# Splitting the fifth expert's weight loads into a quarter, a quarter and a half of the first expert's up projection

## The chip, the cores and the metric

The kernel runs on one core of a Trainium2 chip. The metric is the device time of one execution in microseconds (us); lower is better. Each time is that of the whole program.

## The reference, cut to what matters

A decoder trunk of two layers over 256 tokens of width 1024, all in float32. Each layer is a mixer (gated linear recurrences, retention, a recurrent block) and a mixture of 32 experts; a final norm ends it. The part around the change is the mixture:

```python
def hier_moe(h, w_group, b_group, w_expert, b_expert, w1, w3, w2):
    ...
    top_v, top_i = lax.top_k(e_sel, MOE_TOPK)
    ...
    def expert_step(acc, p):
        w1e, w3e, w2e, ge = p
        hid = jax.nn.silu(xt @ w1e) * (xt @ w3e)
        return acc + ge[:, None].astype(xt.dtype) * (hid @ w2e), None
```

`w1` and `w3` are 1024 x 512 for each expert and `w2` is 512 x 1024, so an expert has 6.29 MB of weights and a layer's 32 experts have 201 MB.

## The kernel before

The two layers run one after the other. In each, the mixer's projections come first, then the final steps of its output projection, the routing (`route`), and then all 32 experts in order (`experts`). Every expert's weights are read from HBM, whatever the number of its tokens. An expert handles its tokens in passes of 32. One pass on TensorE is: gather the tokens (L1235), transpose (L1240, L1244), the up projection with `w1` and `w3` (L1259), the down projection with `w2` (L1275), and the scatter into the sums (L1286 or L1289). ACT and DVE work between these steps.

The up projection of a pass is a loop over eight chunks k of the width, with four calls in each, and each call shows in the trace as two matmul records: 64 records in a pass, 8 for each k. Chunk k reads column block k of `w1` and of `w3`; a whole `w1` is 16 KB in each of 128 partitions, so a half is 8 KB a partition and a quarter is 4 KB.

Weights lie in three slots of SBUF, used in turn. Expert 3 (`FOURTH`, counting from zero) has a place of its own, the memory of `x` and of lent constants, so the slot of expert 0 is next used by expert 4, the fifth (`FOURTH + 1`). All weight loads are issued by one queue, SP's, in an order written by hand: `first_experts` for those that go out during the mixer and the routing, then `load_experts`. There SP waits for a semaphore that tells that the slot was read, and then issues the loads into it. In `load_experts`, SP waits for the routing (`routed`), reads the first expert's token count and works out with `up_to(0)` how many passes there will have been (`done`). Then it waits until the first half of the up projection of that pass is done (`up_half_done`, given at k = 3) and issues the first halves of the fifth's `w1` and `w3`; waits for `up_done` and issues the second halves; waits for `down_done` and issues the fourth expert's `w2`. The next loads are those of expert 5 (L557), after the up projection of expert 1. Of the loop after that, SP's waits are L659 and L662.

Each load adds 16 to a semaphore when it has landed. The up projection waits for the count that `up_count(l, e)` works out; it knows how many loads an expert's weights came in (64 is four loads, 96 is six).

TensorE is kept active ahead of the last expert's up projection by some matmuls on zeros (`keep_warm`, L963), and the last expert's weights come in halves (`last_expert`). The next layer's mixer weights follow behind the last expert in the same queue.

Of the kernel before, what the change touches and what calls it, by code (L numbers as in the profile page):

```python
# [37 lines left out]
KC = D // P  # L38
# [12 lines left out]
PIECE = KC * 512  # L51
# [4 lines left out]
FOURTH = 3  # L56
# [85 lines left out]
def trunk(nc, x_in, even_w_in, even_w_out, odd_w_in, odd_w_out, gla_w_up, rglru_w_r, rglru_w_i,  # L142
# [7 lines left out]
    with ExitStack() as ctx:  # L150
# [3 lines left out]
        def sem(name):  # L154
            return ctx.enter_context(nc.semaphore(name))
# [54 lines left out]
        def up_slot(e):  # L210

            return ORDER[(e - (e > FOURTH)) % 3]

        def w1_place(e):

            return x_place if e == FOURTH else up_slot(e) * SLOT

        def w3_place(e):

            return lent_place if e == FOURTH else up_slot(e) * SLOT + PIECE  # L220
# [222 lines left out]
        got_scaled = sem("got_scaled")  # L443
        spread_turned = sem("spread_turned")
        spread_kept = sem("spread_kept")
        up_done, up_half_done = sem("up_done"), sem("up_half_done")
        fourth_up = Staged(sem("fourth_up"), 48)
        sums_begun = sem("sums_begun")
        silu_done = sem("silu_done")
# [10 lines left out]
        def up_count(l, e):  # L460

            def of(e):
                return 96 if e == 1 else 64 if e == FOURTH + 1 else 32

            same = [j for j in range(NE) if j != FOURTH and up_slot(j) == up_slot(e)]
            return l * sum(map(of, same)) + sum(of(j) for j in same if j <= e)
# [46 lines left out]
        def _(sp_q):  # L513
# [35 lines left out]
            def up_to(e):  # L549

                tokens = sp_q.value_load(counts[0:1, bass.ds(e, 1)], min_val=0, max_val=T)
                with sp_q.Fori(0, tokens, PASS):
                    sp_q.reg_add(passes, passes, 1)
                return sp_q.snap(passes, min_val=1, max_val=2 * NE * T // PASS)
# [9 lines left out]
            def load_half(l, e, src, place, half, loaded):  # L564

                part = slice(half * HALF, (half + 1) * HALF)
                sp_q.dma_start(at_place(place)[:, part], src[l, e].rearrange("(p k) f -> p (k f)", k=KC)[:, part]).then_inc(loaded, 16)
# [56 lines left out]
                sp_q.wait_ge(*((sums_begun, 1) if l == 0 else x_turned.at(1, 4)))  # L624
                load_half(l, FOURTH, moe_w1, x_place, 1, fourth_up.sem)

            def fifth_up(l, half):

                load_half(l, FOURTH + 1, moe_w1, w1_place(FOURTH + 1), half, up_loaded[up_slot(FOURTH + 1)])
                load_half(l, FOURTH + 1, moe_w3, w3_place(FOURTH + 1), half, up_loaded[up_slot(FOURTH + 1)])  # L630

            def load_experts(l):

                sp_q.wait_ge(*routed.at(l, 2))
                done = up_to(0)
                sp_q.wait_ge(up_half_done, done)
                fifth_up(l, 0)
                sp_q.wait_ge(up_done, done)
                fifth_up(l, 1)
                sp_q.wait_ge(down_done, done)  # L640
                load_down(l, FOURTH, ORDER[0])
                for e in (1, 2):
                    done = up_to(e)
                    sp_q.wait_ge(up_loaded[up_slot(e)], up_count(l, e))
                    sp_q.wait_ge(up_done, done)
                    load_up(l, e + 4, e + 4)
                    sp_q.wait_ge(down_loaded[ORDER[e]], down_count(l, e))
                    sp_q.wait_ge(down_done, done)
                    load_down(l, e + 3, ORDER[e])
                done = up_to(FOURTH)  # L650
                sp_q.wait_ge(down_loaded[ORDER[0]], down_count(l, FOURTH))
                sp_q.wait_ge(down_done, done)
                load_down(l, 2 * FOURTH, ORDER[0])
                with sp_q.Fori(0, (NE - 2 - 2 * FOURTH) // 3) as i:
                    for j in range(3):
                        e, like = 3 * i + (2 * FOURTH + 1 + j), 2 * FOURTH + 1 + j
                        done = up_to(3 * i + (FOURTH + 1 + j))
                        sp_q.wait_ge(up_loaded[up_slot(like)], up_count(l, like - 3) + 32 * i)
                        sp_q.wait_ge(up_done, done)  # L659
                        load_up(l, e, like)  # L660
                        sp_q.wait_ge(down_loaded[ORDER[like % 3]], down_count(l, like - 3) + 16 * i)
                        sp_q.wait_ge(down_done, done)  # L662
                        load_down(l, e, ORDER[like % 3])
                last_expert(l, NE - 1, up_to(NE - 4))
# [125 lines left out]
        def _(pe):  # L790
# [425 lines left out]
            def experts(l):  # L1216
# [7 lines left out]
                def expert(e, like, turn, passes):  # L1224
# [5 lines left out]
                    def body(base, n):  # L1230
# [24 lines left out]
                        for k in range(KC):  # L1255
                            if last and k == KC // 2:
                                pe.wait_ge(up_loaded[up_slot(like)], all_up)
                            for j in range(Q):
                                ins = pe.matmul(bank[2][PASS * j:PASS * (j + 1), 0:T], got_T[:, k % 2, k // 2, :],  # L1259
                                                up[:, k, :, j * P:(j + 1) * P], start=(k == 0), stop=(k == KC - 1),  # L1260
                                                tile_position=(0, PASS * j), skip_group_check=True)
                            if k == KC // 2 - 1:
                                ins.then_inc(up_half_done, 1)
                        ins.then_inc(up_done, 1)
# [976 lines left out]
```

## Time and the profile before

| what | value |
|---|---|
| time, median of 3 runs | 1135.0 us (1133.93 to 1135.4) |
| the profiled execution's own time | 1134.56 us |
| its span, first to last instruction | 1132.7 us |
| PE busy | 858.7 us, 76% |
| DVE busy | 354.8 us, 31% |
| ACT busy | 262.2 us, 23% |
| bytes read from HBM | 441.25 MB |
| mean rate over the span | 390 GB/s |
| mean granted clock of TensorE | 0.952 |

How to read it: busy shares are means over stages with different limits. The profiled execution's time is 1.9 us more than its span; that part lies outside the first and last instruction. The 16 DMA engines that move the weights are the resource with the highest share in the slices of the experts' stages.

### The profile page before, as it was taken

The page shows a single profiled execution, that of the slowest core. Times are in us where ns is not written, and L with a number is a line of the kernel's source. Part 1 is how long each engine was busy: PE and PEld are TensorE (multiplying, and loading weights), DVE is VectorE, ACT ScalarE, POOL GpSimd, SP SyncE. Part 2 cuts the span into 40 slices and gives each one's busy share as a digit, 9 for nine tenths or more (in the row PEclk, how much of TensorE's full clock was granted, in tenths as well). Part 3 has the DMA queues.
Part 4 walks back from the last instruction along what each step waited for, and adds up shares of the span by engine and source line. Part 5 has one row for each costly group of instructions (what it writes and reads, how often), then busy time and mean ns, then how long its engine had stood idle before and what let it go on. Part 6 is the DMA issues. An engine that isn't in the chain of part 4 may idle for free.

```text
span 1132.7 us, 25610 instructions
## 1 busy us (share of the span) xinstructions
PE 858.7 (76%) x10392; PEld 543.1 (48%) x10393; DVE 354.8 (31%) x841; ACT 262.2 (23%) x502; POOL 7.4 (1%) x16
## 2 busy tenths in 40 slices
PE   9999997777666666666779998777766666666665
PEld 8988964444333333333349896434433333333333
DVE  6898751212111111111128964121111111111112
ACT  7646541111100000000027744111100000100002
POOL 1000000000000000000001000000000000000000
PEclk9999999999998889999899999999999988988988
DMA  9744899999999999999999599999999999999996
GB/s 345 269 161 179 325 345 426 428 428 428 428 428 430 429 426 430 427 429 428 430 406 368 202 426 378 432 424 428 428 429 429 427 429 429 428 429 428 430 425 250
DMA packets 49901, 442.95 MB, mean 391 GB/s; under 512 B 4288, under 2 KB 5760, under 8 KB 23616
## 3 DMA queue, kind: packets, MB, share of 16 engines
q1 hardware_dynamic: 49584, 441.53, 94.0%
q8 instruction: 32, 0.52, 0.2%
q10 hardware_dynamic: 144, 0.52, 0.1%
q0 software_dynamic: 128, 0.26, 0.1%
q14 instruction: 13, 0.11, 0.0%
HBM read 441.25 MB, written 1.05 MB: 390 GB/s over the span
## 4 chain that ended last, share of the span: by engine, by line
DMA 47%; PE 38%; DVE 7%; ACT 4%; issue 3%; SPq 1%; DVEq 0%; ACTq 0%
DMA up_pairs<-in_moe_w_dram 43%; PE low_banks L1259 13%; PE low_banks L1275 4%; DMA weights<-in_moe_w_dram 4%; PE sums_of_x L812 3%; PE sums_of_x L814 3%; PE sums_of_x L813 3%; PE low_banks L1235 2%; DVE w_lo L1732 1%; PE low_banks L812 1%; PE sums_of_x L1286 1%; PE low_banks L813 1%; PE low_banks L814 1%; PE sums_of_x L1289 1%; PE low_banks L1027 1%
## 5 line engine op out<-in xcount | busy, mean ns | idle before, releaser
L1259 PE MATMUL low_banks<-up_pairs,gates 128*32 128x256 f32 x4096 | 277.4, 431 | 119.7 <-DMA up_pairs<-in_moe_w_dram 106.6
L1259 PEld LDWEIGHTS low_banks<-up_pairs,gates 128*32 128x32 f32 x4096 | 142.4, 123 | 239.1 <-DMA up_pairs<-in_moe_w_dram 116.9
L1275 PE MATMUL low_banks<-weights,gates 128*32 128x256 f32 x2048 | 124.0, 382 | 85.5 <-DVE gates L2153 53.8
L2151 DVE TENSOR_TENSOR gates<-gates,low_banks 128x128 f32<-128x128 f32 x64 | 18.4, 288 | 396.5 <-ACT gates L1321 396.5
L1275 PEld LDWEIGHTS low_banks<-weights,gates 128*32 128x32 f32 x2048 | 63.5, 109 | 145.9 <-issue 85.9
L1321 ACT ACTIVATE gates<-low_banks 128x128 f32<-128x128 f32 x64 | 17.8, 278 | 413.1 <-PE low_banks L1259 413.1
L2147 DVE TENSOR_TENSOR gates<-low_banks,vecs 128x256 f32<-128x256 f32 x64 | 27.2, 425 | 259.5 <-PE low_banks L1244 259.5
L1235 PE MATMUL low_banks<-tok,gates 128*32 128x256 f32 x1024 | 68.5, 385 | 15.0 <-issue 9.5
L1732 DVE TENSOR_TENSOR w_lo<-weights,w_hi 128x2048 fp32r<-128x2048 f32 x28 | 64.0, 2287 | 16.1 <-ACT w_hi L1392 15.9
L1563 ACT COPY gates<-low_banks 128x256 f32<-128x256 f32 x64 | 23.8, 372 | 191.3 <-PE low_banks L1275 191.3
L1557 ACT COPY gates<-low_banks 128x256 f32<-128x256 f32 x64 | 23.8, 372 | 159.2 <-PE low_banks L1235 159.2
L1392 ACT CAST w_hi<-weights 128x2048 fp32r<-128x2048 f32 x28 | 53.4, 1908 | 17.3 <-PE sums_of_x L814 12.2
L1235 PEld LDWEIGHTS low_banks<-tok,gates 128*32 128x32 f32 x1024 | 27.6, 109 | 50.6 <-issue 38.0
L2141 DVE TENSOR_SCALAR gates<-consts,y_T,scale 128x32 f32 x128 | 32.5, 299 | 57.3 <-issue 56.4
L1286 PE MATMUL sums_of_x<-gates 32*128 32x256 f32 x512 | 36.7, 400 | 15.6 <-ACT gates L1563 15.6
L1289 PE MATMUL sums_of_x<-gates 32*128 32x256 f32 x512 | 36.7, 400 | 15.6 <-ACT gates L1563 15.6
L2144 DVE TENSOR_SCALAR gates<-consts,y_T 128x128 f32 x128 | 38.4, 342 | 0.0
L1286 PEld LDWEIGHTS sums_of_x<-gates 32*128 32x128 f32 x512 | 23.1, 184 | 31.7 <-ACT gates L1563 31.0
L1289 PEld LDWEIGHTS sums_of_x<-gates 32*128 32x128 f32 x512 | 23.1, 184 | 31.7 <-ACT gates L1563 31.0
L1244 PE MATMUL low_banks<-consts,gates 128*128 128x128 f32 x128 | 28.0, 300 | 7.6
L812 PE MATMUL sums_of_x<-act_hi,w_hi 128*128 128x256 f32 x112 | 32.3, 288 | 1.0 <-DVE w_lo L1732 1.0
L812 PE MATMUL sums_of_x<-w_hi,act_hi 128*128 128x512 f32 x80 | 32.4, 404 | 0.0
(296 smaller groups left out, 1124.0 us busy)
## 6 DMA issues: line engine op xcount, KB each, us to landing
up_pairs<-in_moe_w_dram SPq DMA_DIRECT2D x114, 2048.0 KB, 33.6
weights<-in_moe_w_dram SPq DMA_DIRECT2D x60, 2048.0 KB, 39.6
up_pairs<-in_moe_w_dram SPq DMA_DIRECT2D x24, 1024.0 KB, 10.0
weights<-in_even_w_in_dram SPq DMA_DIRECT2D x5, 2048.0 KB, 11.2
weights<-in_odd_w_in_dram SPq DMA_DIRECT2D x4, 2048.0 KB, 21.6
weights<-in_moe_w_dram SPq DMA_DIRECT2D x6, 1024.0 KB, 38.0
up_pairs<-in_moe_w_dram SPq DMA_DIRECT2D x8, 512.0 KB, 9.0
weights<-in_even_w_in_dram SPq DMA_DIRECT2D x3, 1024.0 KB, 10.1
```

What stands on the lines that cost most here:

```text
L812: pe.matmul(dst, a_hi, b_hi, start=start, stop=False, skip_group_check=shared)
L813: pe.matmul(dst, a_hi, b_lo, start=False, stop=False, skip_group_check=shared)
L814: return pe.matmul(dst, a_lo, b_hi, start=False, stop=stop, skip_group_check=shared)
L1235: ins = pe.matmul(bank[0][PASS * q:PASS * (q + 1), 0:T], pick[:, a, :], tok[:, a, q * T:(q + 1) * T], start=(a == 0), stop=(a == TT - 1), ...
L1259: ins = pe.matmul(bank[2][PASS * j:PASS * (j + 1), 0:T], got_T[:, k % 2, k // 2, :], up[:, k, :, j * P:(j + 1) * P], start=(k == 0), stop= ...
L1275: ins = pe.matmul(bank[3][PASS * q:PASS * (q + 1), T:2 * T], hid_T[:, c, :], down[:, c, q * T:(q + 1) * T], start=(c == 0), stop=(c == Q - 1),
L1286: ins = pe.matmul(dst, y_tok[rows, part], spread_T[rows, :], start=False, stop=True, tile_position=(PASS * q, 0), skip_group_check=True)
L1289: ins = pe.matmul(dst, spread_T[rows, part], y_tok[rows, :], start=False, stop=True, tile_position=(PASS * q, 0), skip_group_check=True)
L1392: act.copy(hi, raw_w).then_inc(hi_set.sem, splits_of(l, i))
L1732: tt(lo, raw_w, hi.bitcast(F32), ALU.subtract).then_inc(lo_set.sem, splits_of(l, i))
L2141: ts(pick[:, a, :], numbers, place[:, a, bass.ds(e, 1)], scale[:, a:a + 1], ALU.is_equal, ALU.mult).then_inc(picked, 1)
L2144: ts(spread[:, a, :].rearrange("p (q s) -> p q s", q=Q), numbers.unsqueeze(1).to_broadcast([P, Q, PASS]), place[:, a, bass.ds(e, 1)], gate ...
```

## The change

The first expert's slot is given back in three parts and not in two. TensorE signals a new semaphore, `up_quarter_done`, at the end of chunk k = 1 of every pass, on a matmul that is there already. SP waits for it and issues the first quarter of the fifth expert's `w1` and `w3`, then waits for `up_half_done` and issues the second quarter of both, then for `up_done` and issues the second half of both. The bytes are the same: six loads (four of 512 KB, two of 1024 KB) instead of four of 1024 KB. `up_count` counts 96 for the fifth expert. This holds for both layers.

```diff
-        up_done, up_half_done = sem("up_done"), sem("up_half_done")
+        up_done, up_half_done, up_quarter_done = sem("up_done"), sem("up_half_done"), sem("up_quarter_done")
...
-                return 96 if e == 1 else 64 if e == FOURTH + 1 else 32
+                return 96 if e == 1 else 96 if e == FOURTH + 1 else 32
...
-            def fifth_up(l, half):
-
-                load_half(l, FOURTH + 1, moe_w1, w1_place(FOURTH + 1), half, up_loaded[up_slot(FOURTH + 1)])
-                load_half(l, FOURTH + 1, moe_w3, w3_place(FOURTH + 1), half, up_loaded[up_slot(FOURTH + 1)])
+            def fifth_up(l, first, last):
+
+                e = FOURTH + 1
+                part = slice(first * PIECE // KC, last * PIECE // KC)
+                for src, place in ((moe_w1, w1_place(e)), (moe_w3, w3_place(e))):
+                    sp_q.dma_start(at_place(place)[:, part], src[l, e].rearrange("(p k) f -> p (k f)", k=KC)[:, part]
+                                   ).then_inc(up_loaded[up_slot(e)], 16)
...
                 done = up_to(0)
+                sp_q.wait_ge(up_quarter_done, done)
+                fifth_up(l, 0, KC // 4)
                 sp_q.wait_ge(up_half_done, done)
-                fifth_up(l, 0)
+                fifth_up(l, KC // 4, KC // 2)
                 sp_q.wait_ge(up_done, done)
-                fifth_up(l, 1)
+                fifth_up(l, KC // 2, KC)
                 sp_q.wait_ge(down_done, done)
...
+                            if k == KC // 4 - 1:
+                                ins.then_inc(up_quarter_done, 1)
                             if k == KC // 2 - 1:
                                 ins.then_inc(up_half_done, 1)
```

## Rows read from the trace of the kernel before

**Rows 1.** The page: bytes moved in 40 equal slices of 28.3 us.
```profile
GB/s 345 269 161 179 325 345 426 428 428 428 428 428 430 429 426 430 427 429 428 430 406 368 202 426 378 432 424 428 428 429 429 427 429 429 428 429 428 430 425 250
```

**Rows 2.** The page: the chain that ended last, by engine.
```profile
DMA 47%; PE 38%; DVE 7%; ACT 4%; issue 3%; SPq 1%; DVEq 0%; ACTq 0%
```

**Rows 3.** The chain in order of time: start us, us, what.
```profile
163.92 3.66 PE low_banks L1259 x64
...
276.58 3.70 PE low_banks L1259 x64
280.93 36.00 DMA up_pairs<-in_moe_w_dram
...
697.81 3.66 PE low_banks L1259 x64
...
803.07 33.17 DMA up_pairs<-in_moe_w_dram
...
1060.86 39.65 DMA up_pairs<-in_moe_w_dram
1100.55 5.97 PE low_banks L1259 x64
```

**Rows 4.** Timeline of SP's queue, load issues: start us, us, line, count.
```profile
147.00 0.89 SPq L597 DMA_DIRECT2D up_pairs<-in_moe_w_dram  x2
...
165.91 2.71 SPq L567 DMA_DIRECT2D up_pairs<-in_moe_w_dram  x4
...
167.64 0.98 SPq L567 DMA_DIRECT2D up_pairs<-in_moe_w_dram  x2
...
170.76 0.33 SPq L574 DMA_DIRECT2D weights<-in_moe_w_dram  x1
178.71 1.48 SPq L557 DMA_DIRECT2D up_pairs<-in_moe_w_dram  x2
...
699.80 2.74 SPq L567 DMA_DIRECT2D up_pairs<-in_moe_w_dram  x4
...
712.51 0.80 SPq L557 DMA_DIRECT2D up_pairs<-in_moe_w_dram  x2
```

**Rows 5.** Windows, layer 0: length, engines' busy us, clock, DMA share, GB/s.
```profile
165.00:165.50 0.50, 0.50 (x16) 0.31 (x12) 0.00 (x0) 0.00 (x0) 0.00 (x0) 1.00 0.64 246
165.50:166.00 0.50, 0.50 (x16) 0.33 (x12) 0.00 (x0) 0.00 (x0) 0.00 (x0) 1.00 0.00 0
166.00:166.50 0.50, 0.50 (x16) 0.28 (x11) 0.00 (x0) 0.00 (x0) 0.00 (x0) 1.00 0.00 0
...
166.50:169.00 2.50, 1.30 (x25) 0.58 (x21) 0.69 (x2) 0.28 (x1) 0.00 (x0) 1.00 0.80 226
```

**Rows 6.** Windows, layer 1, the same columns.
```profile
699.00:699.50 0.50, 0.50 (x16) 0.30 (x12) 0.00 (x0) 0.00 (x0) 0.00 (x0) 1.00 0.55 229
699.50:700.00 0.50, 0.50 (x18) 0.27 (x10) 0.00 (x0) 0.00 (x0) 0.00 (x0) 1.00 0.24 98
700.00:700.50 0.50, 0.50 (x16) 0.33 (x12) 0.00 (x0) 0.00 (x0) 0.00 (x0) 1.00 0.23 98
...
700.50:703.00 2.50, 1.30 (x28) 0.61 (x24) 0.69 (x2) 0.28 (x1) 0.00 (x0) 1.00 0.85 239
```

**Rows 7.** Windows of longer stretches, the same columns.
```profile
154.00:157.00 3.00, 3.00 (x25) 2.90 (x25) 2.17 (x17) 2.87 (x5) 0.00 (x0) 1.00 1.05 405
147.00:150.00 3.00, 3.00 (x25) 2.34 (x25) 2.08 (x4) 1.26 (x2) 0.00 (x0) 1.00 1.03 434
165.50:178.70 13.20, 10.70 (x172) 5.65 (x164) 2.13 (x7) 1.41 (x5) 0.00 (x0) 1.00 0.89 357
699.50:712.50 13.00, 10.57 (x172) 5.57 (x160) 2.13 (x7) 1.41 (x5) 0.00 (x0) 1.00 0.94 371
189.60:277.00 87.40, 65.67 (x1000) 35.12 (x1004) 17.05 (x56) 10.91 (x32) 0.00 (x0) 1.00 1.01 427
...
178.70:181.70 3.00, 1.91 (x32) 1.13 (x32) 1.71 (x6) 0.23 (x1) 0.00 (x0) 1.00 1.02 431
```

**Rows 8.** Windows of the next-to-last expert's up projection in layer 1.
```profile
1100.50:1106.50 6.00, 5.91 (x64) 2.62 (x64) 0.00 (x0) 0.00 (x0) 0.00 (x0) 0.61 0.98 412
...
1115.90:1119.70 3.80, 3.72 (x66) 1.98 (x64) 0.00 (x0) 0.01 (x1) 0.00 (x0) 1.00 0.77 319
```

## The prediction

> **What bounds the kernel now.** I read the slices of the page first: from slice 7 on the core takes in 424 to 432 GB/s, nearly without a break, until layer 0's experts end, and again in layer 1 [rows 1]. That is the level of the DMA engines when they are full: 427 GB/s at a share of 1.01 over 87 us [rows 7]. The chain's summary says the same, 47% of the span for DMA against 38% for PE [rows 2]. The chain in order of time shows where which of the two holds: in layer 0 it runs on PE from the first expert until 280 us and then from one landing of weights to the next, and so in layer 1 from 803 us [rows 3]. The PE part of that chain is not a limit of its own. The stream of weights is full through it, and what the last landings wait for is the number of bytes ahead of them. So any time in which the DMA engines stand still after the stream has begun is paid again at each layer's end, and only such time can be won. There is one such hole in each layer, just where the change is made: in layer 0 the rate falls to 246 and then to 0 GB/s for a full microsecond [rows 5]; in layer 1 to 98 GB/s at a share of 0.24 for a microsecond, some engines still having work [rows 6]. Both end some 0.9 us after SP's four issues begin, at 165.91 and 699.80 us [rows 4].
>
> **The change part by part.**
>
> The moved issue. The four issues start when half of the first expert's up projection is done; the next two, which wait for its end, start 167.64 − 165.91 = 1.73 us later [rows 4]. Those 1.73 us are four chunks of k, so two chunks are 0.87 us, and the first quarter goes out at about 165.04 and 698.93 us. The up projection itself takes 3.66 us in both layers, one pass [rows 3], a quarter of which is 0.92 us; I take 0.87. SP is free by then: it has only been waiting. It issues two loads in 0.89 us [rows 4] (the pair at 147.00), so it is done at about 165.93 and comes some 0.02 us late to the half, nothing that counts, because 1.05 MB (2.5 us of transfer) is then ahead; the second half's issue stays at 167.64. Layer 0's hole, where all engines are idle, shortens by the full 0.87 us, as the first bytes follow their issue by the same time.
>
> In layer 1 a share of 0.24 of the engines is still busy with old work in the hole. An engine that has no idle time wins nothing by the earlier issue, and an expert's weights are there only when the slowest engine has brought its part. The bounds are 0.2 us (the slowest engine, with the little idle time that it has at the hole's end) and 0.87 us. I take 0.5 us, since the laggards can catch up during the slow restart of the others.
>
> The restart. After a hole the stream does not come back at once: 226 GB/s over 2.5 us in layer 0, 239 GB/s in layer 1 [rows 5, 6]; against 427 that is 2.5 × (427 − 226) = 0.50 MB, or 1.2 us, and 1.1 us. It remains as it is, only earlier. What the trace doesn't show is a restart with rows of 4 KB. If it went by rows and not by bytes, the first part would lose up to half of what is moved in its first microseconds, some 0.3 MB, 0.7 us; from below it costs nothing, since the slow start would be one in time. The nearest rows speak for the low end: transfers of 512 KB issued at 147.00, of rows of 8 KB, run at 434 GB/s, and a stretch of 2 KB rows at 405 [rows 7]. Between these, 2 × 1.05 MB in 4 KB rows costs at most (427/405 − 1) × 4.9 = 0.27 us; I take 0.15 us a layer for all of it.
>
> The next refill. SP's next loads, those of expert 5, go out at 178.71 and 712.51 us, set by PE, which the change doesn't move [rows 4]. From the hole's end to there 6.29 MB are issued; 13.2 × 357 = 4.71 MB were moved in layer 0 and 13.0 × 371 = 4.82 MB in layer 1 [rows 7], so 1.5 MB are left, 3.5 us of work. With the change it is some 0.7 us less, 2.8 us. A new issue needs 0.9 us for its first bytes and about 3 us until the full rate (165.91 to 169). So the queue is then just about as short as that. Before, nothing is to be seen there, 431 GB/s behind 178.70 [rows 7]. Bounds: nothing, or the whole of what was won. I take 0.15 us a layer. From expert 6 on the queue grows with each expert, since PE takes 11 us an expert that needs 14.7 us of transfer, and nothing more can be lost.
>
> TensorE's new signal sits on a matmul that is there, and costs nothing; two more waits and two more issues (0.8 us) on SP hide behind the first expert's up projection. Were that cover gone, 0.8 us of SP time would delay the loads behind it by as much.
>
> The sum: layer 0 0.87 − 0.15 − 0.15 = 0.57; layer 1 0.50 − 0.15 = 0.35 after the rows' cost, and I take no further refill cost there, because its queue is some tenths fuller. Together 0.9 us. The layers add up, since the mixer of layer 1 starts from layer 0's last landing. Against the profiled execution that is 1134.56 − 0.9 = 1133.7 us, and against the median of the runs, which is 0.4 us more, 1135.0 − 0.9 = 1134.1 us.
>
> **The rivals.**
>
> *It is given back at the next refill.* The queue runs short behind 178.71 us and a dip like the restart's (up to 1.1 us) eats what was won, 0.7 us a layer. For it: 2.8 us of work against a start of 3 us. Against it: half of that start already moves bytes. It gives 1135.0 us, and up to 0.4 us more.
>
> *The clock at the end gives more.* The next-to-last expert's up projection in layer 1 took 5.97 us, where 3.66 us is usual, for the granted clock was 0.61 of full over it, which is half its time or more at 1.2 GHz and the rest at 2.4, after a wait for weights [rows 3, 8]. It lies on the chain behind the last wait. If an earlier landing meets the full clock there, up to 2.3 us come on top: 1135.0 − 0.9 − 2.3 = 1131.8 us. For it: that it now has the longest time shown; against it: PE waits there as long as before, so it will most likely be slow again.
>
> *Each transfer pays a restart, so it gets slower.* If the 1.15 us of a slow start belong to each transfer and not to the hole, two more in each layer cost 2.3 us; with 0.15 for the rows and 0.87 won it is 1.6 us a layer, 3.2 in all: 1138.2 us. It beats the gain from 0.36 us a transfer, and makes the kernel slower by 0.2% from 0.93 us. Against it: 434 GB/s over the 512 KB transfers of 147 to 150 us, which stand behind others in the queue [rows 7].
>
> The Trainium skill, in "DMA: Bandwidth & Descriptors", section "Bandwidth", tells to batch loads to 1 MiB or more, and its section on the anatomy of one DMA gives about 2.0 us of fixed cost for each on GpSimd's path. By that, four more transfers would be 8 us, if none overlapped, and the estimate would be 1135.0 + 8 − 1.7 = 1141 us. By that rule the trace disagrees for queued transfers of half that size, with the 434 GB/s just named; for a first transfer after a hole no run here shows it yet.
>
> **How the numbers follow.** What a measurement of this kernel can tell from no change is about 0.2%, 2.3 us. The forecast, 1134.1 us, has 0.66; given back 0.14 (1135.0 to 1135.4); the clock 0.14 (1131.8); a restart for each transfer 0.06 (1138.2). So faster 0.14, within 0.2% 0.80, slower 0.06. The range for 8 in 10 leaves out the last and the far end of the clock's case: the bounds of the sum give 1135.0 − 1.74 = 1133.3 to 1135.4 us, the runs spread over 1.5 us by themselves, and half of the clock's case comes in: 1132.3 to 1135.7 us.
>
> **What would show it.** In the profile after: SP's issues for the fifth at about 165.0 and 698.9 us, in three pairs; the hole of layer 0 shorter by 0.87 us, and that of layer 1 gone for the busy engines; the rate behind 178.7 us at 430 GB/s (right) or below 400 for a microsecond (given back); the first landing behind 280 us earlier by 0.6 us and layer 0's last by as much, layer 1's by 0.9 us. The prediction is wrong if the first microseconds at 4 KB rows move half the bytes, if the next refill dips, or if the up projection at 1100 us runs at another clock.

## The result and the profile after

The changed kernel takes 1137.4 us (median of 9 runs, 1135.96 to 1140.32), the kernel before 1135.0 us (9 runs, 1133.49 to 1136.42). The ratio is 1.0023 with a 95% interval of 1.0013 to 1.0032: slower by 0.23%, 2.6 us (the two medians are 2.4 us apart). Forecast were 1134.1 us, and a range of 1132.3 to 1135.7 us.

The page of the changed kernel, its span and the bytes moved in 40 slices of 28.4 us:

```profile
span 1135.8 us, 25614 instructions
...
GB/s 344 267 163 178 329 336 417 427 426 429 428 428 429 428 429 428 429 428 429 428 407 359 190 426 362 430 426 428 426 430 428 427 430 426 430 428 427 430 425 261
```

Beside [rows 1] the slices with the first experts are lower: 336 and 417 GB/s for 345 and 426 in layer 0, 362 for 378 in layer 1. Behind them both streams are full. (359 and 190 for 368 and 202 lie between the layers' experts.) So the bytes that were lost were lost around the fifth expert's loads.

A measure that other stages disturb less than the whole time is the stretch from the start of a layer's first up projection to that of its next-to-last expert, which starts when its weights land. Timeline of PE, the kernel before in layer 0 (its other three starts are in [rows 3]):

```profile
566.76 3.66 PE L1259 MATMUL low_banks<-up_pairs,gates 128*32 128x256 f32 x64 [2.36 <-DMA up_pairs<-in_moe_w_dram]
```

The same four starts in the changed kernel (the line is now L1264):

```profile
164.00 3.66 PE L1264 MATMUL low_banks<-up_pairs,gates 128*32 128x256 f32 x64 [0.52 <-DVE gates L2154]
...
569.21 3.66 PE L1264 MATMUL low_banks<-up_pairs,gates 128*32 128x256 f32 x64 [2.47 <-DMA up_pairs<-in_moe_w_dram]
...
701.43 3.66 PE L1264 MATMUL low_banks<-up_pairs,gates 128*32 128x256 f32 x64 [0.52 <-DVE gates L2154]
...
1104.56 4.96 PE L1264 MATMUL low_banks<-up_pairs,gates 128*32 128x256 f32 x64 [2.35 <-DMA up_pairs<-in_moe_w_dram]
```

Layer 0's stretch grew from 566.76 − 163.92 = 402.84 to 569.21 − 164.00 = 405.21 us, so by 2.4 us; layer 1's from 1100.55 − 697.81 = 402.74 to 403.13 us, by 0.4 us. Together 2.8 us, close to the 2.6 us of the timed runs. The rest of the profiled execution nearly cancels: between 566.76 and 697.81 us it took 1.2 us more, with a granted clock of 0.61 over the 3 us from 697 us on, just ahead of layer 1's first up projection, where it had been full, and behind 1100.55 us 0.9 us less, since the slow up projection there took 4.96 us and not 5.91. Both are single executions. The three stretches of a layer that an experiment left as before came out within 0.13 us of 402.84 and 402.74 (below); the change in layer 0, traced in two kernels, gave +2.4 and +2.7 us.

Where the 2.4 us went shows in windows of 2.5 us. The kernel before, behind its holes, with the next ones after those of [rows 5] and [rows 6] (columns as there):

```profile
169.00:171.50 2.50, 2.02 (x36) 1.24 (x32) 1.01 (x4) 0.37 (x1) 0.00 (x0) 1.00 0.99 419
171.50:174.00 2.50, 2.31 (x35) 1.08 (x28) 0.00 (x0) 0.46 (x2) 0.00 (x0) 1.00 1.00 423
...
703.00:705.50 2.50, 2.02 (x40) 1.23 (x35) 1.02 (x4) 0.37 (x1) 0.00 (x0) 1.00 0.99 419
```

The changed kernel, layer 0 and then layer 1:

```profile
166.50:169.00 2.50, 1.30 (x28) 0.59 (x24) 0.69 (x2) 0.28 (x1) 0.00 (x0) 1.00 0.89 252
169.00:171.50 2.50, 2.02 (x36) 1.18 (x35) 1.02 (x4) 0.37 (x1) 0.00 (x0) 1.00 0.72 208
171.50:174.00 2.50, 2.37 (x34) 1.13 (x30) 0.00 (x0) 0.37 (x2) 0.00 (x0) 1.00 1.01 369
703.50:706.00 2.50, 1.59 (x32) 0.68 (x24) 0.49 (x2) 0.28 (x1) 0.00 (x0) 1.00 0.94 262
706.00:708.50 2.50, 1.93 (x32) 1.12 (x32) 1.21 (x5) 0.21 (x1) 0.00 (x0) 1.00 0.91 256
708.50:711.00 2.50, 2.29 (x33) 1.31 (x34) 0.00 (x0) 0.19 (x2) 0.00 (x0) 1.00 1.07 436
```

Before, the stream was at 419 GB/s 3 us after the issue. Now it stays at 208 to 262 GB/s for 5 us, and in layer 0 at 369 after that. In layer 0 the share of busy DMA engines falls to 0.72 from 169.00 us on, when SP is already on the last of its six issues; so some engines had nothing to do although there was work.

SP's queue in the changed kernel, layer 0 (the first pair, then the second half), and for layer 1 the first four:

```profile
165.13 1.79 SPq L632 DMA_DIRECT2D up_pairs<-in_moe_w_dram  x2
...
167.92 1.50 SPq L632 DMA_DIRECT2D up_pairs<-in_moe_w_dram  x2
...
702.57 1.76 SPq L632 DMA_DIRECT2D up_pairs<-in_moe_w_dram  x4
```

The first issue came where it was forecast, 1.13 us behind the up projection's start. But in layer 0 the first pair took 1.79 us, as much as four issues in layer 1: the second alone took 1.40 us against 0.42. Over just that time the DMA queues' view shows a packet of another kind (queue, packets, MB, share):

```profile
q8 instruction: 1, 0.02, 5.5%
```

It is a block of instructions of 16 KB. By the trace's records it is on the wire from 165.60 to 166.56 us, and SP's second issue, begun at 165.52, ends at 166.92. In the kernel before the same packet passes from 165.20 to 166.17 us. SP's first issue there, at 165.91, falls into it and takes 0.33 us as elsewhere; the second, at 166.30, comes behind it.

### The profile page after: what moved, and what is told of

Read it like the earlier page. It is cut to its first block, busy times and chain, and to the rows that moved or that the text cites. A ratio compares the mean times of both kernels' runs of the same rounds, so it can differ in the third digit from the quotient of the medians.

```text
span 1135.8 us, 25614 instructions
## 1 busy us (share of the span) xinstructions
PE 862.7 (76%) x10392; PEld 544.5 (48%) x10393; DVE 355.0 (31%) x841; ACT 262.2 (23%) x502; POOL 7.2 (1%) x16
## 4 chain that ended last, share of the span: by engine, by line
DMA 48%; PE 37%; DVE 7%; ACT 4%; issue 3%; SPq 2%; DVEq 0%; ACTq 0%
DMA up_pairs<-in_moe_w_dram 44%; PE low_banks L1264 12%; PE low_banks L1282 4%; PE sums_of_x L817 3%; DMA weights<-in_moe_w_dram 3%; PE sums_of_x L818 3%; PE sums_of_x L819 3%; PE low_banks L1240 2%; DVE w_lo L1739 1%; PE low_banks L817 1%; PE sums_of_x L1293 1%; PE low_banks L819 1%; PE low_banks L818 1%; PE sums_of_x L1296 1%; PE low_banks L1032 1%
## 5 line engine op out<-in xcount | busy, mean ns | idle before, releaser
L1264 PE MATMUL low_banks<-up_pairs,gates 128*32 128x256 f32 x4096 | 280.4, 435 | 118.9 <-DMA up_pairs<-in_moe_w_dram 106.4
L1264 PEld LDWEIGHTS low_banks<-up_pairs,gates 128*32 128x32 f32 x4096 | 143.5, 124 | 240.3 <-DMA up_pairs<-in_moe_w_dram 116.1
L1249 PE MATMUL low_banks<-consts,gates 128*128 128x128 f32 x128 | 28.3, 303 | 7.4
```

## The experiments

All were compared with the kernel before, run on the same chip. The table has for each what its profile gave for the two stretches, as the difference to before's 402.84 us (layer 0) and 402.74 us (layer 1), and the ratio of the times. The ratios are known to 0.1% (1.1 us) only: outside the two stretches the traced executions of all these kernels differ by 3.7 us. Each stretch, on the other hand, is of one execution.

Two more columns tell the stream as a whole from its slowest part. A load is moved by 16 DMA engines and adds 16 to its semaphore, and the trace has these 16 increments one by one; they are taken here as one for each engine. An up projection can start only with the last of them. From six loads of `w2` in each layer, 130 us and more behind the first up projection, the columns give by how much the mean of the 16 came later than before, measured from that up projection. The last of the 16 came later by as much as the stretch grew, to 0.2 us. The mean is steady: from the first loads behind the edit to the layer's end it keeps its distance, and in the three layers left as before it is within 0.1 us. What the stretch has beyond the mean is the slowest engine, fallen further behind the others.

Before, the 16 increments of a load were spread over 2.0 us (layer 0) and 2.2 us (layer 1), in the changed kernel over 4.2 and 2.6 us. So of the 2.4 us of layer 0 the stream as a whole lost 1.1, and the slowest engine the rest. Not all of that part is made at the edit: in layer 1 of three_eighths the mean is as before and the last increment 0.2 us earlier at 60 us behind the first up projection, but 0.7 us later at 75 us; in layer 0 of early_halves it is 0.7 us earlier at 45 us and 0.2 us later at 65 us; in layer 1 of early_all_quarters it is 0.3 us later at 70 us and 1.0 at 75 us. The edits are at 1 to 5 us. Why an engine falls back there is open, and a difference of less than 1 us between two stretches need not be the edit's.

| kernel | stretch, layer 0, us | stretch, layer 1, us | mean of the 16, layer 0, us | mean of the 16, layer 1, us | time ratio (95% interval) |
|---|---|---|---|---|---|
| the change | +2.4 | +0.4 | +1.1 | +0.2 | 1.0023 (1.0013 to 1.0032) |
| layer0_only | +2.7 | −0.1 | +0.9 | 0.0 | 1.0016 (1.0004 to 1.0027) |
| layer1_only | 0.0 | +0.2 | +0.1 | +0.1 | 1.0008 (0.9999 to 1.0017) |
| late_quarters | +0.9 | +1.2 | +0.8 | +0.9 | 1.0022 (1.0012 to 1.0031) |
| early_halves | +0.1 | −0.4 | −0.2 | −0.7 | 1.0000 (0.9991 to 1.0009) |
| late_halves | +0.5 | +0.7 | +0.8 | +0.9 | 1.0019 (1.0009 to 1.0029) |
| alternate_rows | +0.9 | +1.0 | +0.4 | +0.4 | 1.0009 (1.0001 to 1.0018) |
| by_partitions | +4.6 | +5.7 | +4.9 | +5.1 | 1.0087 (1.0073 to 1.0101) |
| quarter_then_rest | +0.9 | −0.2 | +0.5 | −0.4 | 1.0019 (1.0010 to 1.0029) |
| three_eighths | +0.8 | +1.0 | +0.4 | 0.0 | 1.0008 (0.9999 to 1.0017) |
| early_all_quarters | +2.2 | +1.1 | +1.2 | +0.3 | 1.0036 (1.0023 to 1.0049) |
| shifted_after | +0.4 | +0.4 | 0.0 | 0.0 | 1.0018 (1.0008 to 1.0027) |
| shifted_early_halves | 0.0 | −0.4 | −0.1 | −0.7 | 1.0006 (0.9997 to 1.0015) |
| layer1_gap | +0.1 | +1.2 | +0.1 | +0.8 | 1.0018 (1.0007 to 1.0028) |
| full_queue_quarters | +1.6 | +0.8 | +1.1 | +0.7 | 1.0010 (1.0001 to 1.0018) |
| full_queue_halves | +0.3 | +0.2 | +0.2 | +0.2 | 0.9999 (0.9990 to 1.0009) |
| full_queue_fourths_of_rows | 0.0 | −0.1 | 0.0 | 0.0 | 1.0005 (0.9996 to 1.0014) |

### Taking the change apart: its transfers, its earlier start

late_quarters has the transfers and not the start:

```diff
-                sp_q.wait_ge(up_quarter_done, done)
+                sp_q.wait_ge(up_half_done, done)
                 fifth_up(l, 0, KC // 4)
```

> The fifth expert's first halves are issued at the half, as before, but as four transfers of 512 KB in 4 KB rows instead of two of 1024 KB. Only rows and number of transfers differ from before. Measure beside the time: from the start of the first up projection to the first one that waits for a landing, 153.05 us before and 155.63 us after in layer 0, 138.47 and 138.81 us in layer 1. Theory R (4 KB rows make the restart slower): layer 0 at 155.5 to 156.5 us, the time 2 to 4 us above before, at least as slow as the changed kernel, since the gain of the earlier start is gone too. Theory S (the early start itself harms, by meeting a queue that is not yet empty): layer 0 at 153 us, no change in the time.

Measured 1137.59 us against 1135.24, ratio 1.0022; the stretches +0.9 and +1.2 us, the means +0.8 and +0.9. Without any early start the time is as slow as with the whole change, so the theory of the early start as the only culprit falls. But the landing that theory R put at 155.5 to 156.5 us came at 154.02 (153.05 before): the transfers alone make less than half of layer 0's 2.4 us. Its windows in layer 0, from the first bytes:

```profile
169.00:171.50 2.50, 1.30 (x28) 0.61 (x24) 0.69 (x2) 0.28 (x1) 0.00 (x0) 1.00 0.83 215
171.50:174.00 2.50, 2.02 (x40) 1.23 (x35) 1.01 (x4) 0.37 (x1) 0.00 (x0) 1.00 0.98 298
174.00:176.50 2.50, 2.34 (x36) 1.12 (x28) 0.00 (x0) 0.60 (x2) 0.00 (x0) 1.00 1.06 438
```

The first window is as slow as before's (226 GB/s), the second moves 298 GB/s where before's moved 419, at nearly the same busy share. That is 2.5 × 121 = 0.3 MB, 0.7 us.

early_halves has the start and not the transfers. The first expert's up projection leaves out chunks 2 and 3 (the count that the up projection waits for goes along and is not shown):

```diff
                 sp_q.wait_ge(up_quarter_done, done)
-                fifth_up(l, 0, KC // 4)
-                sp_q.wait_ge(up_half_done, done)
-                fifth_up(l, KC // 4, KC // 2)
+                fifth_up(l, 0, KC // 2)
...
-                                                up[:, k, :, j * P:(j + 1) * P], start=(k == 0), stop=(k == KC - 1),
+                                                up[:, k + 4 if like == 0 and k in (2, 3) else k, :, j * P:(j + 1) * P], start=(k == 0), stop=(k == KC - 1),
```

> The first expert's up projection leaves out chunks 2 and 3 and reads chunks 6 and 7 in their place (its result is another one, its time the same), so that the whole first half of its slot is free at a quarter of the up projection. The fifth expert comes in the four transfers of the kernel before, the first two 0.87 us earlier. Theory R: an early start with 8 KB rows wins what was forecast, 0.6 to 1.7 us below before, layer 0 at 152.2 to 152.5 us. Theory S: slower than before, layer 0 at 154 us or more.

Measured 1135.66 us, ratio 1.0000. In layer 1 the mean of the engines won 0.7 us of the 0.87, and the slowest 0.4. In layer 0 the mean won 0.2, and the stretch nothing (+0.1): 153.31 us for the landing, where theory R had 152.2 to 152.5 and theory S 154 or more. In layer 0 SP's first pair took 1.69 us here too:

```profile
165.65 1.69 SPq L632 DMA_DIRECT2D up_pairs<-in_moe_w_dram  x2
```

So an earlier start with long rows is worth 0.4 us where SP is not held up. late_halves goes the other way: before's transfers, the first pair at k = 5 (`if k == 3 * KC // 4 - 1`).

> The kernel before with the fifth expert's first halves issued at chunk k = 5, 0.87 us later than before. If idle time of the stream counts one to one, both layers' landings come 0.87 us later and the time is 1.7 us above before. If the length of the restart takes it up, as the gain of an earlier start was taken up, less than half of that.

The stretches grew by 0.5 and 0.7 us for 0.87 us of delay; the time ratio, 1.0019, is 2.2 us with an interval of 1.0 to 3.3. For the mean of the engines the idle time counts one to one (+0.8 and +0.9 us). For the last increment, which a landing waits for, it does not: the spread of the 16 shrank from 2.0 and 2.2 us to 1.8 and 1.9.

quarter_then_rest issues the quarter early and the other three quarters, in rows of 12 KB, when the up projection is done.

> A quarter at the quarter (two transfers in 4 KB rows), then the other three quarters when the up projection is done (two transfers in 12 KB rows): four transfers in each layer, as before, half as many 4 KB rows as in the changed kernel. Theory R: between before and the changed kernel, layer 0 at 153.5 to 155 us; 1.05 MB must last from 165.0 to 168.6 us, and may run out for 0.3 us. Theory N: at most before's time. Theory S: as the changed kernel.

Layer 0 +0.9, layer 1 −0.2 us (means +0.5 and −0.4). The sum of the stretches, 0.7 us, would be a ratio of 1.0006; the measured 1.0019 has an interval from 1.0010 on, so here the one traced execution does not stand for the timed runs. Layer 1 gained with half the 4 KB rows; in layer 0 SP's second issue was held up again, 1.15 us.

### One layer at a time

```diff
-                sp_q.wait_ge(up_quarter_done, done)
-                fifth_up(l, 0, KC // 4)
-                sp_q.wait_ge(up_half_done, done)
-                fifth_up(l, KC // 4, KC // 2)
+                if l == 0:
+                    sp_q.wait_ge(up_quarter_done, done)
+                    fifth_up(l, 0, KC // 4)
+                    sp_q.wait_ge(up_half_done, done)
+                    fifth_up(l, KC // 4, KC // 2)
+                else:
+                    sp_q.wait_ge(up_half_done, done)
+                    fifth_up(l, 0, KC // 2)
```

> The change in layer 0 alone; layer 1 as before. Theory R (each layer pays about 0.9 us for the 4 KB rows at the restart, and the earlier start wins 0.9 us only where the issues are not held up): in layer 0 SP's second issue meets an instruction packet and takes 1.3 us or more, so layer 0 wins nothing from the earlier start: 1.0 to 2.5 us above before. Theory E (both layers pay the same): half of the whole change, 1.2 us above.

> The change in layer 1 alone. Theory R: price and gain cancel, within 0.5 us of before, its first landing after the PE-bound stretch 138.4 to 138.9 us behind the first up projection (138.43 before). Theory E: 1.2 us above before.

layer1_only has `l == 1` in its place. Measured ratios 1.0016 and 1.0008. The stretches are sharper: +2.7 and −0.1 us for the one, 0.0 and +0.2 us for the other. The loss is in layer 0, and both layers' values repeat those of the whole change (+2.4, +0.4) to 0.3 us.

early_all_quarters brings the second half as quarters too.

> The changed kernel with the second half too as four transfers of 512 KB in 4 KB rows: eight transfers for each layer. Theory R (a price for transfers in short rows): a further 0.5 to 1 us a layer, 1 to 2 us above the changed kernel, 3.5 to 4.5 above before. If the price is only that of the restart, the second half costs nothing further but its lower rate, 0.1 us.

1138.8 us (5 runs), ratio 1.0036. Layer 1's stretch went from +0.4 to +1.1 us, but its last increment fell back by 0.7 us only between 70 and 75 us, far behind these loads; layer 0 stayed at +2.2. By the means, 1.2 and 0.3 us for 1.1 and 0.2, the second half's quarters cost some 0.1 us a layer, as the expectation's last sentence has it. The price is not one for each transfer alone. Why the time is 1.4 us above the changed kernel's the trace doesn't tell.

### Is it the number of transfers or the length of their rows?

by_partitions and alternate_rows issue the first half at the old time as four transfers of 512 KB with 8 KB rows, the first for 64 partitions in a block, the second for every second partition:

```diff
+                    sp_q.dma_start(at_place(place)[first:first + P // 2, 0:HALF],
+                                   src[l, e].rearrange("(p k) f -> p (k f)", k=KC)[first:first + P // 2, 0:HALF]
...
+                    sp_q.dma_start(at_place(place)[first::2, 0:HALF],
+                                   src[l, e].rearrange("(p k) f -> p (k f)", k=KC)[first::2, 0:HALF]
```

> At the half, four transfers of 512 KB as in late quarters, but each of 64 partitions with rows of 8 KB. Theory R: as before within 0.5 us, layer 0 at 153 us. Theory N (a price for each further transfer, whatever its rows): as late quarters, 1 us or more above before in layer 0.

> At the half, four transfers of 512 KB with rows of 8 KB, each for every second partition, so that each still reaches all parts of SBUF and the transfers differ from late quarters only by the length of their rows and by having 64 of them. Theory R (the rows): as before within 0.7 us, the queue 3.9 us long when SP issues expert 5's loads. Theory N (the number of transfers): as late quarters, 2.4 us above before, the queue 4.8 us long there.

by_partitions was 10 us slower, for a reason of its own. Its window while such transfers were on the way:

```profile
171.00:176.00 5.00, 4.36 (x67) 2.35 (x60) 1.01 (x4) 0.93 (x3) 0.00 (x0) 1.00 1.03 218
```

All DMA engines are busy, and move half of what they do elsewhere: with transfers into 64 neighbouring partitions the rate is 218 GB/s. It tells nothing on rows. alternate_rows does. Its windows in layer 0, from the first bytes:

```profile
167.00:169.50 2.50, 1.30 (x28) 0.61 (x23) 0.69 (x2) 0.28 (x1) 0.00 (x0) 1.00 0.76 203
169.50:172.00 2.50, 2.02 (x40) 1.23 (x34) 1.02 (x4) 0.37 (x1) 0.00 (x0) 1.00 0.99 403
```

The second window moves 403 GB/s, near before's 419, where the 4 KB rows of late_quarters moved 298. So the rate behind the hole goes by the length of the rows. The means say the same: +0.4 and +0.4 us with 8 KB rows, +0.8 and +0.9 with 4 KB rows. Yet the stretches are +0.9 and +1.0 us, nearly those of late_quarters, since the slowest engine fell back further (a spread of 2.8 us in both layers for 2.0 and 2.2). So neither theory holds alone: four transfers in place of two cost the stream 0.4 us a layer whatever their rows, the shorter rows about as much again, and the slowest engine made up the difference here. The kernel is not a clean test of the number: its four issues took 0.58 us each, and its first bytes came later.

Next, away from the hole. The kernel before with expert 6's up weights, for which 8 us of work stand ahead in the queue, in parts:

```diff
-                    load_up(l, e + 4, e + 4)
+                    if e == 2:
+                        for quarter in range(4):
+                            part = slice(quarter * PIECE // 4, (quarter + 1) * PIECE // 4)
+                            for src, place in ((moe_w1, w1_place(6)), (moe_w3, w3_place(6))):
+                                sp_q.dma_start(at_place(place)[:, part], src[l, 6].rearrange("(p k) f -> p (k f)", k=KC)[:, part]
+                                               ).then_inc(up_loaded[up_slot(6)], 16)
```

full_queue_halves has two parts of 8 KB rows in place of the four; full_queue_fourths_of_rows has eight transfers too, each of every fourth partition (`[quarter::4]`) with rows of 16 KB.

> The kernel before, but expert 6's up weights, issued with some 8 us of work in the queue, come in eight transfers of 512 KB in 4 KB rows instead of two of 2048 KB. Theory R with a full queue: only the lower rate of 4 KB rows, 420 instead of 432 GB/s over 4.2 MB, 0.3 us a layer, not to be told from before in the time. Theory N: six further transfers at 0.45 us each, 2.7 us a layer, 5 us above before.

> The kernel before with expert 6's up weights as four transfers of 1024 KB in 8 KB rows. Theory rows: a price between that of 16 KB rows (none) and of 4 KB rows (340 GB/s over 5 us, 1 us a layer): 0.3 us a layer or less. Theory number: two further transfers cost a third of the six of full_queue_quarters, also 0.3 us; the two are told apart by the next kernel.

> The kernel before with expert 6's up weights as eight transfers of 512 KB, each of every fourth partition with its whole row of 16 KB. Theory rows: the rate stays above 415 GB/s through these transfers. Theory number: it falls to about 340 GB/s for 5 us as in full_queue_quarters, 1 us a layer.

The windows in which these transfers pass, first that of the kernel before, with two transfers in 16 KB rows:

```profile
198.00:203.00 5.00, 3.80 (x76) 2.22 (x71) 1.22 (x5) 0.28 (x1) 0.00 (x0) 1.00 0.99 416
```

Then 4 KB rows:

```profile
198.00:203.00 5.00, 3.80 (x76) 2.12 (x68) 0.69 (x2) 0.28 (x1) 0.00 (x0) 1.00 0.98 340
203.00:208.00 5.00, 4.18 (x64) 2.23 (x56) 1.02 (x4) 0.98 (x3) 0.00 (x0) 1.00 1.02 419
```

8 KB rows:

```profile
198.00:203.00 5.00, 3.80 (x74) 2.13 (x70) 0.69 (x2) 0.28 (x1) 0.00 (x0) 1.00 1.01 418
```

And 16 KB rows, eight transfers:

```profile
198.00:203.00 5.00, 3.80 (x72) 2.20 (x68) 0.93 (x4) 0.28 (x1) 0.00 (x0) 1.00 1.01 426
```

With the queue full, the number costs nothing (426 GB/s, means and stretches within 0.1 us of before), and the row does: against the whole rows' 426 GB/s the 4 KB rows lose 5 × (426 − 340) = 0.43 MB, 1.0 us, in their first 5 us, and then run at 419. The means are +1.1 and +0.7 us, the stretches +1.6 and +0.8; the time ratio, 1.0010, is 1.1 us with an interval of 0.1 to 2.0. Both theories were off, with 0.3 and 2.7 us a layer. 8 KB rows can't be told from whole rows by these windows (418 for before's 416); their means are +0.2 us. Since 4 KB rows pay as much here as at the hole, "a price for the restart with 4 KB rows", as theory R had it, was half the truth.

By the Trainium skill, "DMA: Bandwidth & Descriptors", section "Bandwidth", transfers should be of 1 MiB or more. For the full queue the trace disagrees, as eight of 512 KB run at 426 GB/s; for the hole it agrees, with 0.9 and 1.0 us more in the stretches of alternate_rows.

three_eighths issues 3/8 of both matrices (6 KB rows) at k = 2, and the rest, in 10 KB rows, at the end.

> Three eighths of both matrices (rows of 6 KB) when three of eight chunks are done, 0.43 us sooner than before's halves, and the other five eighths (rows of 10 KB) when all are done: four transfers as before. Theory rows: the shorter rows cost some 0.3 to 0.5 us a layer and the start wins 0.4 us at most: within 0.7 us of before. It beats before only if 6 KB rows cost nothing, then by 0.4 to 0.9 us.

Ratio 1.0008; stretches +0.8 and +1.0 us, means +0.4 and 0.0. No gain, and no kernel tried here beats the kernel before.

### Why layer 0 lost more: the held-up issue

shifted_after and shifted_early_halves put 72 waits that are long met into TensorE's program at an idle place:

```diff
+                for _ in range(72):
+                    pe.wait_ge(pool_set, 2)
                 pe.wait_ge(*y_ready.at(0, 8))
```

> The changed kernel with 72 further waits in TensorE's program, all met long before, where TensorE stands idle in layer 0's mixer. They move the 16 KB instruction packet that TensorE needs during the first expert's up projection (1.6 us behind its start in the changed kernel, on the wire for 1 us) to before it. Theory C (in layer 0 SP's second issue meets this packet and is held up for 1 us, which costs what the earlier start wins and more): SP's second issue takes 0.43 us instead of 1.40, layer 0's landing comes 153.5 to 154.5 us behind the first up projection instead of 155.6, the time about 1.5 us below the changed kernel. Theory R alone (only the rows cost, the packet nothing): landing at 155 us or more, the time as that of the changed kernel.

> Early halves (chunks 2 and 3 of the first expert's up projection left out for 6 and 7) with the same 72 waits. Theory C: layer 0 wins as layer 1 did (landing 0.4 us sooner than before there), so at 152.3 to 152.7 us instead of 153.25, the time 1 us below before. Theory R alone: as early halves.

The edit did not do what it was for: the instruction packet did not move ahead of the up projection, but came 0.3 us later behind its start (1.9 us instead of 1.6). By luck that moved it from SP's second issue to its third. shifted_after's SP queue in layer 0, the first pair and the third:

```profile
167.30 0.80 SPq L632 DMA_DIRECT2D up_pairs<-in_moe_w_dram  x2
...
168.16 1.62 SPq L632 DMA_DIRECT2D up_pairs<-in_moe_w_dram  x1
```

Now the first pair takes 0.80 us and the third issue 1.62, and the stretch is +0.4 us instead of +2.4. The mean is as before (0.0). So it is not just that SP is held up; it matters that the second transfer, `w3`'s first quarter, comes 1 us late, just when the queue has run out. This is one execution. In shifted_early_halves the second issue was hit again (1.80 us) and layer 0 won nothing again in the stretch (mean −0.1). The time of shifted_after doesn't bear the 2 us out: its ratio, 1.0018, is an interval of 0.9 to 3.1 us, and its two stretches sum to 0.8; where the packet fell in its other runs is not known.

That the packet holds the issue up is seen in the times. In all eight kernels with an early start in layer 0 the packet passes while SP issues, and one issue is long. In six of them the long issue ends 0.36 or 0.37 us after the packet does, whether the packet ends 2.30 or 2.85 us behind the up projection's start; in the two shifted kernels 0.80 and 0.82 us after. In four kernels whose second issue in layer 0 began 0.07 to 0.26 us before the packet's end (late_quarters, layer1_gap, full_queue_quarters, full_queue_fourths_of_rows) that issue ends 0.36 or 0.37 us after it too. The first issue of a group is not held up: that of the kernel before took 0.33 us inside the packet's time. In layer 1 no packet is near, and the second issue takes 0.42 or 0.43 us in every kernel where it follows the first at once, but for the two with issues of half the partitions.

layer1_gap makes such a gap in layer 1, where no packet is near: layer1_only, with `w3`'s first quarter held until chunk k = 4.

```diff
                     sp_q.wait_ge(up_quarter_done, done)
-                    fifth_up(l, 0, KC // 4)
-                    sp_q.wait_ge(up_half_done, done)
+                    fifth_up(l, 0, KC // 4, (0,))
+                    sp_q.wait_ge(up_five_done, done)
+                    fifth_up(l, 0, KC // 4, (1,))
                     fifth_up(l, KC // 4, KC // 2)
```

> layer1_only with the second transfer of the first quarter (w3's) held back until five chunks of the up projection are done, about 0.9 us later than it was, and the second quarter's two behind it. Theory C (what made layer 0 slow is the held-up second issue): layer 1's first landing after the PE-bound stretch comes 139.8 to 140.5 us behind the first up projection instead of 138.64. Theory L (something else of layer 0): 139.2 us or less, what is late by the bytes alone being made up by the queue.

Layer 1 went from +0.2 to +1.2 us (mean +0.1 to +0.8), and the landing came at 139.56 us: the gap alone costs 0.9 us, between the two theories' values. Its windows:

```profile
701.00:703.50 2.50, 2.35 (x44) 1.17 (x36) 0.00 (x0) 0.08 (x1) 0.00 (x0) 1.00 0.82 249
703.50:706.00 2.50, 1.45 (x28) 1.12 (x32) 1.62 (x6) 0.20 (x1) 0.00 (x0) 1.00 0.82 220
706.00:708.50 2.50, 2.02 (x36) 1.03 (x29) 0.09 (x1) 0.37 (x1) 0.00 (x0) 1.00 0.92 346
```

It is the picture of the change's layer 0: a second slow window at a reduced busy share, and a third one below 370 GB/s. The change's layers differ by 2.0 us in the stretch and 1.0 us in the mean. The gap explains half of the first and two thirds of the second; the rest stays open.

## Why the prediction was wrong, point by point

What bounds the kernel held: the stream of weights is full from the fifth expert on, and the two stretches, 2.8 us longer together, are of the size of the whole result. The hole was the right place to look.

The moved issue came at 165.13 us for a forecast 165.04, and 1.14 us behind the up projection's start in layer 1. "SP issues two loads in 0.89 us" was wrong in layer 0, where it took 1.79.

"Layer 0's hole shortens by the full 0.87 us", and that this is won, failed. With before's own transfers an earlier start won 0.4 us in layer 1 (0.5 forecast) and nothing in layer 0. The reason that the prediction gave for layer 1, that a landing waits for the slowest engine, is the right one, and it holds in layer 0 too: the mean of the engines won 0.7 us in layer 1 and lost 0.8 and 0.9 by a delay of 0.87, the last increment only 0.4, and 0.5 and 0.7 in the stretches.

**The step that failed** is the cost of the restart in short rows, the term "I take 0.15 us a layer for all of it", from bounds of nothing and 0.7 us. By late_quarters it is 0.9 and 1.2 us (0.8 and 0.9 in the mean), above the upper bound. The row that it was taken from was misread. SP's queue and a window of the kernel before:

```profile
144.12 0.80 SPq L567 DMA_DIRECT2D up_pairs<-in_moe_w_dram  x2
...
152.00:154.00 2.00, 1.87 (x15) 1.25 (x15) 1.58 (x5) 0.29 (x1) 0.00 (x0) 1.00 0.93 281
```

The 434 GB/s of 147 to 150 us are the two transfers of 1024 KB in 8 KB rows that were issued at 144.12. Those of 512 KB issued at 147.00 (L597) are in pieces of 2 KB, and their packets come from 152 us on: at 281 GB/s for 2 us, and only then at the 405 of [rows 7]. Against 427 that start loses 0.3 MB, 0.7 us. So the nearest row for short pieces that start spoke for the prediction's upper bound, not for its low end.

The refill was right for the rate: 434 GB/s behind 178.80 us, no dip. The queue was longer, not shorter, since the stream was behind. But in layer 0 the last increment, 1.5 us later than before for the fourth expert's `w2`, was 2.8 us later for expert 5's first load, with the mean the same 1.2 us; in layer0_only it was 3.3 us later already at that `w2`. What makes it is open.

The rivals: the clock's case did happen in part (the up projection behind the last wait took 4.96 us) and was cancelled by a slow clock elsewhere; how often it happens in the other runs, they don't tell. "Each transfer pays a restart", 1138.2 us with a chance of 0.06, was the nearest in the time, but too dear and without the rows: two more transfers in a layer cost 0.9 to 1.2 us at the hole, where it had said 2.3, and by the means about half of that is the rows. It was set aside with the misread row, which has no 512 KB transfers in it. That such transfers cost nothing with a full queue, full_queue_fourths_of_rows did show later; the mistake was then to carry it over to an empty one.

With the measured terms the sum of the means is, in layer 1, −0.7 for the start + 0.9 for the transfers = 0.2 us, which is what the change has there. In layer 0 it is −0.7 + 0.8 + 0.6 for the late second issue (layer1_gap) = 0.7 us of 1.1, so 0.4 are open. The slowest engine adds 1.3 and 0.2 us to the measured 1.1 and 0.2, which makes the 2.8.

Open: why more transfers cost anything at the hole; why 4 KB rows are slow only for their first 5 us in a full queue; what makes the slowest engine fall back, and with it half of layer 0's excess. That the instruction packet causes the long issues rests on their times alone, since no kernel had layer 0's early start without it.

## What to carry to other kernels

When a queue has run empty, restart it with few and large transfers. Cutting the first one up to start it 0.9 us sooner cost more (0.9 to 1.2 us a layer) than the start could win (0.4 us), and a second transfer that came 0.9 us late cost another 0.9 us. Count the length of the contiguous rows at the hole and in a full queue; the number of transfers only at the hole: in the full queue eight transfers with whole rows were free, and 4 KB pieces of 16 KB rows lost 0.7 to 1.1 us. A landing waits for the slowest of the 16 engines, so read the mean of the increments and their last one; they can move apart. Take the price of an edit at a stage's edge from rows of such an edge, not from the steady run, and make sure which transfers are on the wire in a window: here those issued 3 us before it.

## What the runs showed of the hardware

- SP's first issue behind a wait took 0.33 us and the next mostly 0.42 to 0.45; one that was under way while a 16 KB instruction packet passed took 1.15 to 1.80 us (1.40 in the changed kernel's layer 0) and ended 0.36 us after the packet in six of eight kernels. Issues of 0.6 to 1.2 us are also seen without a packet, at the end of a group of four or more (1.01 us in layer 1 of layer1_gap).
- The 16 increments of one load were spread over 2.0 us in the kernel before and 4.2 us in the changed one (layer 0), and a landing waits for the last.
- Transfers of 8 KB rows into 64 neighbouring partitions ran at 218 GB/s with all DMA engines busy; into every second partition they ran at 403.
- 4 KB pieces of 16 KB rows: 340 GB/s for 5 us and then 419, 8 KB pieces 418, whole rows 416 and 426, all with a full queue in layer 0.
- Times of one kernel differ by 3 to 5 us (before: 1133.68 to 1138.55 us in one set of 33 runs). Outside the two stretches the traced executions differ by 3.7 us, while the stretches left as before repeat to 0.13 us. But one trace is one execution: in quarter_then_rest, shifted_after and full_queue_quarters the two stretches lie outside what the timed runs allow.
